# A transformer block pair on one core: later loads in the opening, and two layer-norm steps moved

## The reference, cut to what matters

```
h    = rmsnorm(x, ln_g);  proj = h @ w_in          # g_u g_v g_z | d_q d_k d_v d_z d_a d_b | c_q c_z
v    = layernorm(gelu(g_v), ln_g, ln_b)            # per position, 512 wide
s    = tril(W_s) v + b, per chunk of 128 positions and group
outa = gelu(g_u) * s * silu(g_z)
outb = rmsnorm(gated_delta_rule(q, k, v, g, beta)) * silu(d_z)          # 8 heads
m    = rmsnorm(mem, mem_norm_g);  mk, mv = m @ w_mem_kv                 # 256 memory positions
outc = softmax(c_q mk^T / sqrt(128)) mv * silu(c_z)                     # 4 heads
x    = x + [outa, outb, outc] @ w_out;  rmsnorm
```

## Time and profile before

| | us |
|---|---|
| median of 3 runs | 1923.31 (1923.17 to 1923.55) |
| the profiled execution, its own time | 1925.46 |
| its span | 1923.9 |
| PE busy | 1912.3 (99%) |
| DVE busy | 1150.7 (60%) |
| ACT busy | 816.1 (42%) |
| PE's share of the chain that ended last | 94% |
| HBM read | 193.10 MB, 105 GB/s over the span |

### The profile page before, as it was taken

One profiled execution on the slowest core, in us unless ns is written; L12 is line 12 of the kernel. 1 busy time (PEld: TensorE's weight loads), 2 busy tenths in 40 slices (PEclk: granted clock), 3 DMA queues, 4 the chain that ended last, 5 costly groups with the idle time before them and its releaser, 6 DMA issues.

```text
span 1923.9 us, 27478 instructions
## 1 busy us (share of the span) xinstructions
PE 1912.3 (99%) x9142; PEld 1590.7 (83%) x9142; DVE 1150.7 (60%) x2161; ACT 816.1 (42%) x1603; POOL 112.1 (6%) x172
## 2 busy tenths in 40 slices
PE   9999999999999999999999999999999999999999
PEld 8788888888888888888888888888888888888887
DVE  6574587788777765633655555555464646466333
ACT  5653444444444434523544343434343434344111
POOL 0100011001111010001000000000000000000100
PEclk9999999999999999999999999999999999999999
DMA  9722233223332213344332222222222222223341
GB/s 339 274 91 67 86 89 90 75 75 79 88 84 73 69 66 120 121 143 144 128 108 79 87 93 87 93 87 93 87 83 97 71 100 79 88 88 120 142 153 65
DMA packets 33737, 202.09 MB, mean 105 GB/s; under 512 B 4576, under 2 KB 4704, under 8 KB 13216
## 3 DMA queue, kind: packets, MB, share of 16 engines
q1 hardware_dynamic: 23760, 165.69, 24.2%
q0 software_dynamic: 9792, 35.76, 6.6%
q10 hardware_dynamic: 144, 0.10, 0.0%
HBM read 193.10 MB, written 8.42 MB: 105 GB/s over the span
## 4 chain that ended last, share of the span: by engine, by line
PE 94%; DVE 3%; DMA 2%; ACT 1%; issue 0%; SPq 0%; POOL 0%; DVEq 0%; ACTq 0%
PE gemm L1472 80%; PE pb L1472 12%; PE pb L1475 2%; DMA raw<-in_w 2%; DVE w_lo L823 1%; DVE act_lo L832 0%; ACT w_hi L392 0%; DVE scratch L864 0%; DVE scratch L1033 0%; DVE scratch L959 0%; DVE stat L953 0%; DVE scratch L952 0%; DVE parts L843 0%; DVE scratch L960 0%; ACT scratch L561 0%
## 5 line engine op out<-in xcount | busy, mean ns | idle before, releaser
L1472 PE MATMUL gemm<-act_hi,w_hi 128*128 128x512 f32 x2304 | 920.9, 400 | 0.2 <-DVE act_lo L832 0.2
L1472 PE MATMUL gemm<-act_lo,w_hi 128*128 128x512 f32 x2320 | 902.8, 389 | 0.2 <-DVE w_lo L823 0.2
L1472 PE MATMUL gemm<-act_hi,w_lo 128*128 128x512 f32 x2304 | 899.8, 391 | 0.0
L392 ACT ACTIVATE w_hi<-raw 128x512 fp32r<-128x512 f32 x616 | 337.0, 619 | 409.4 <-PE gemm L1472 385.9
L1472 PEld LDWEIGHTS gemm<-act_hi,w_lo 128*128 128x128 f32 x2304 | 432.4, 188 | 93.2
L1472 PEld LDWEIGHTS gemm<-act_lo,w_hi 128*128 128x128 f32 x2320 | 436.6, 188 | 83.7 <-ACT w_hi L392 0.5
L1472 PEld LDWEIGHTS gemm<-act_hi,w_hi 128*128 128x128 f32 x2304 | 433.4, 188 | 82.0 <-issue 0.8
L823 DVE TENSOR_TENSOR w_lo<-raw,w_hi 128x512 fp32r<-128x512 f32 x624 | 399.3, 695 | 142.7 <-ACT w_hi L392 135.7
L1472 PEld LDWEIGHTS pb<-scratch 128*128 128x128 f32 (+1 forms) x932 | 135.9, 190 | 31.6 <-DVE scratch L1194 5.9
L1472 PE MATMUL pb<-scratch 128*128 128x128 f32 (+4 forms) x932 | 144.9, 281 | 3.0 <-DVE scratch L838 1.8
L1342 DVE SCALAR_TENSOR_TENSOR scratch<-gemm,scratch 128x512 f32<-128x512 f32 x24 | 16.6, 691 | 150.1 <-PE gemm L1472 149.9
(11 more groups left out here) (293 smaller groups left out, 1603.2 us busy)
## 6 DMA issues: line engine op xcount, KB each, us to landing
raw<-in_w SPq DMA_DIRECT2D x154, 1024.0 KB, 4.8
scratch<-in_rows_in POOLq DMA_DIRECT2D x6, 1024.0 KB, 8.6
big<-in_xT POOLq DMA_DIRECT2D x4, 1024.0 KB, 9.4
scratch<-rows POOLq DMA_DIRECT2D x16, 256.0 KB, 6.1
scratch<-in_xT POOLq DMA_DIRECT2D x16, 256.0 KB, 3.0
x<-big POOLq DMA_DIRECT2D x16, 256.0 KB, 2.3
scratch<-x POOLq DMA_DIRECT2D x16, 256.0 KB, 4.1
outT<-scratch POOLq DMA_DIRECT2D x16, 256.0 KB, 3.7
```

Of the source, the lines that this page charges most:

```text
L392: A(w_hi[slot][:, c], raw[slot][:, c], ACT.Copy).then_inc(sem["hi"], 1)
L1472: return nc.tensor.matmul(out, a, b, start=start, stop=stop, skip_group_check=skip)
```

## The change

In POOL's opening the constants go from the end of memory block 4 (`unit` 5) to that of block 5; row copy 1 from block 4 to block 6; row copy 2 from block 5 to block 7; x's part 0 from block 6 to block 7. ACT squares row copy 1 after the conversion of unit 9 and not before that of x tiles 6 and 7; it squares copy 2 after x tiles 8 to 11, and copy 3 after the conversion of unit 10. DVE finishes the layer norm of chunks 1 and 2 after the cross-attention heads, between the steps of chunk 3.

```diff
 (POOL)
             pool.wait_ge(sem["unit"], 4)
             x_part(3)
-            pool.wait_ge(sem["unit"], 5)
+            pool.wait_ge(sem["unit"], 6)
+            pool.dma_start(cst[:, :], consts).then_inc(sem["cst_in"], 16)
+            pool.wait_ge(sem["unit"], 7)
             x_rows(1)
-            pool.dma_start(cst[:, :], consts).then_inc(sem["cst_in"], 16)
-            pool.wait_ge(sem["unit"], 6)
+            pool.wait_ge(sem["unit"], 8)
+            x_part(0)
             x_rows(2)
-            pool.wait_ge(sem["unit"], 7)
-            x_part(0)
             x_rows(3)
             x_part(1)
 (ACT)
             hi(7, 1)
             x_hi(4, 6)
             hi(U_V, 0)
-            row_squares(1)
             x_hi(6, 8)
             hi(U_V + 1, 1)
+            row_squares(1)
+            x_hi(8, 12)
             row_squares(2)
-            x_hi(8, 12)
+            hi(U_V + 2, 0)
             row_squares(3)
             act.wait_ge(sem["cst_in"], 16)
             row_scales(MT, MT + XT, XT)
-            hi(U_V + 2, 0)
             x_hi(12, KT)
 (DVE)
             v_norm(0)
             lo(U_X + 1, (U_X + 1) % 2)
             v_mean(2)
-            v_norm(1)
-            v_norm(2)
 ...
             v_poly(3)
+            v_norm(1)
             v_mean(3)
+            v_norm(2)
             v_norm(3)
```

## The result

| | before | after |
|---|---|---|
| median of 20 runs | 1923.01 us | 1926.94 us |
| lowest and highest | 1921.10, 1926.84 | 1922.38, 1928.26 |
| ratio of the times | | 1.0017 (1.0011 to 1.0023) |
| the profiled execution's span | 1923.9 | 1924.8 |

The change costs 0.17%, 3.3 us by the ratio, where 4.9 were to be won. It is outside the range and of the other sign. The two profiled executions lie 0.9 us apart; the runs further. I come to that difference with the second traces.

What follows compares the result with a forecast made beforehand. PE, busy 99% of the span, was taken to bound the kernel, so only its idle or slow time could be won. -5.24 + 1.7 - 1.4 = -4.9 us gave 1918.4 us, range 1916.4 to 1921.3.

Steps and rivals of the forecast that it cites:

- Term 1: Opening: memory block 7's wait and the slow clock behind it vanish, unit 8 starts at 53.79 not 59.03; -5.24 us.
- Term 2: Memory's scales: `negatives` issued at 73.9, not 72.50, lands later and makes PE wait; +1.7 us (0 to 3.4).
- I get 60: POOL's queue: row copy 3, waiting for ACT to square copy 1, is issued at 60.
- (b): Memory's scales: wait returns at about 3.4 us, clock may fall with it; -1.6 us, 1921.7; chance 0.13.
- (c): Copy 3 lands late; PE waits 1.7 us at x's scales, 6.1 at memory's, clock slows; +2.8, 1926.1; chance 0.06.
- Term 3: Layer norm moved off DVE before the first cross-attention head, so c_q comes sooner; -1.4 us (other end -0.7).
- (d): Opening: tile 7 stays late because something other than POOL's loads held it; -1.4 us, 1921.9; chance 0.05.
- (e): Block 7's clock drop has a cause other than the standstill; -4.9 + 1.65 us, 1920.1; chance 0.05.

Runs made afterwards that it cites:

- the second traces: One more profiled execution each of the unedited kernel before (span 1922.3 us) and the unedited changed kernel (span 1921.2 us).
- opening alone: The changed kernel with the layer-norm move undone: 1926.00 us, ratio 1.0019 to the kernel before.
- sums later: The changed kernel with ACT's wait for the small loads and its copy of the sums moved behind the conversion of unit 11: 1920.49 us, ratio 0.9990.
- ACT's old order: The changed kernel with ACT's squares at their places in the kernel before, POOL as changed: 1921.74 us, ratio 0.9998.
- sums later, ACT's old order: The changed kernel with ACT's small-load wait and sums copy behind unit 11's conversion, and ACT's squares ordered as before: 1920.52 us, ratio 0.9984.
- layer norm alone: The kernel before with only the layer-norm move: 1921.35 us, ratio 0.9996.
- the first experiments: The earlier of the follow-up kernels, timed beside the kernel before; the text doesn't list which ones.
- row copy 1 alone: The kernel before with only row copy 1 moved, from the end of memory block 4 to that of block 5: one trace, no times compared.

## Why the prediction was wrong

**Term 1, -5.24 us: the mechanism right, the size wrong.** Tile 7 landed 7.3 us after its issue in place of 11.75 (4.8 to 8.8 in all nine traces of the new opening, 9.7 to 11.7 in the four of the old one), block 7 follows block 6 without idling in every trace of the new opening, and unit 8 started at 56.0 and 54.5 in the two traces of the changed kernel. Two things were mis-sized. The base: I took the 3.42 us and the 1.65 us of slow clock of one execution for those of the median run, though its time, 1925.46, stood 2.15 us above the median, as I wrote, and put the sum on the median alike. The second trace shows 1.91 us and no slow clock. And the other end: the tiles of blocks 4 and 6, which the change doesn't touch, landed up to 2.4 us later than in the first trace, so 53.8 was reached only once. From first trace to first trace term 1 is 59.03 - 55.98 = 3.05 us, from second to second 57.18 - 54.53 = 2.65.

**Term 2, +1.7 us: the step that failed.** The place was named and so was the mechanism, but `negatives` was not issued at "73.9": it went out at 78.71, and at 76.77 in the second trace. What that number left out is the landing of row copy 2, for which the sum has no time. It lets the conversion of unit 10 (2.2 us) end at 69 behind copy 2's square (1.9 us), so it takes copy 2 to have landed by 69 - 2.2 - 1.9 = 64.9, within 10.6 us of its issue at 54.3. Copy 2 landed 13.0 us after its issue, at 70.2 (12.5 us, at 68.2, in the second trace), and it was issued later because unit 8 was late. In the traces of the new loads:

| kernel | ACT's squares | unit 8 | copy 2 issued | its square starts | last memory copy issued | `negatives` issued |
|---|---|---|---|---|---|---|
| forecast | new | 53.8 | 54.3 | | 71.8 | 73.9 |
| after, first trace | new | 55.98 | 57.16 | 70.21 | 76.61 | 78.71 |
| after, second trace | new | 54.53 | 55.74 | 68.20 | 74.66 | 76.77 |
| opening alone | new | 55.46 | 56.68 | 69.32 | 75.87 | 77.98 |
| sums later | new | 55.26 | 56.48 | 67.34 | 74.40 | 76.50 |
| ACT's old order | old | 53.75 | 54.96 | 65.73 | 72.37 | 74.48 |
| sums later, ACT's old order | old | 54.78 | 56.00 | 67.03 | 73.68 | 75.78 |

In each of them ACT stands waiting for copy 2 until it lands, and the last memory copy goes out 6.4 to 7.1 us after that square starts, in either order. "I get 60" for copy 3 was too early as well (65.19, 63.40), since copy 1's square stood behind the conversion of unit 9, whose tile landed only at 60.7. But that did not decide: in the kernel with the sums later, with the same order on ACT, copy 3 went out at 59.91, and `negatives` still at 76.50.

ACT's order has a part in it. Counted from the start of unit 8, `negatives` goes out 21.2 to 22.7 us later in the new order and 20.7 and 21.0 in the old, where I had 20.1. The times say that the old order is cheaper (0.9998 against 1.0017); why copy 2 landed sooner in it, after 9.8 to 11.0 us against 10.9 to 13.0, no run shows.

The wait was 3.0 to 3.2 us in the three traces of the new order in which the small loads are issued last and ACT waits for them, near the end of 3.4 that I had given. The forecast counts nothing for the clock behind that wait, which only (b) and (c) did; in two of the three it fell, and cost 1.7 and 3.0 us more.

**Term 3, -1.4 us: right.** Head 0 goes from 27.20 to 25.87 us in the changed kernel, and to 25.88 with the layer norm alone. The moved instructions are hidden: the gating products start at 230.38, with no idling listed before them, 118.4 us after unit 12 against 119.8 in the first trace.

**The rivals.** What happened is (b), and in the size of (c): the wait came back at the memory's scales with the slow clock. (c) had its place wrong, since x's scales never stopped PE, and its copy wrong: it was copy 2, not copy 3, that landed nearly as late as the constants had (13.0 us after its issue, against 13.9). But what followed from it, `negatives` at 78.3, is what was measured (78.71). I gave the two 0.19 together, because I weighed (b) by the middle of a landing time and took the issue time as known. (d) falls: tile 7 came sooner. (e), that the clock drop has another cause than idling, is neither shown nor needed: while PE had work, 0.50 was seen behind idling of 3.42, 3.19, 3.18 and 2.4 us, and never without; but 2.96 and 1.9 us left it at 1.00, so the length of the wait alone doesn't tell.

**The sum once more**, from first trace to first trace at unit 12: -3.05 (unit 8) + 3.5 (92.73 - 55.98 against 92.26 - 59.03) + 1.7 (clock) = +2.2; head 0 gives 1.33 back, and the spans differ by +0.9, as they do. From second to second: 108.53 - 107.94 = +0.6 at unit 12, 226.92 - 227.80 = -0.9 at the gating products, and the spans differ by -1.1. So the traces lie +0.9 and -1.1 apart where the runs lie +3.3 apart, by the ratio: most runs of the changed kernel must lose more than these traces show, as with the slow clock of the trace with the opening alone. The mean granted clock over the span, kept for each run, points the same way: it is 0.998 or 0.999 in 18 of the 20 runs of the changed kernel, the two at 1.000 are its two shortest, and in the 29 runs of the kernel before that were made beside the first experiments it is 1.000 in 23 and never 0.998. Which stretch was slow in which run was not traced.

## What to carry to other kernels

A load that is moved later takes with it every wait that stands behind it on in-order queues, so before moving one, list what shares its semaphore and what is queued behind that wait: here a copy whose result PE first reads about 150 us later (at 234.2, with the copy at 87.45) held the scales that PE was about to need, and moving two lines was worth 5.2 us. Where an engine's work is reordered to follow later loads, follow the chain load, square, slot free, next load to its end, and give every load in it a landing time, and the worst of the trace and not the middle one. And don't take the size of a stall from a single profile when that profile is dearer than the median: trace it twice.

## What the runs showed of the hardware

PE's clock adds a second cost to a wait, and not always. Waits of 2.96 and 3.19 us at the same place differ by 0.2 us, yet the first left the granted clock at 1.00 and the second was followed by 0.50 (1.2 GHz) and cost 1.7 us more; with the opening alone 3.18 us of idling were followed by 0.50 for twice as long, which cost 3.0 us; and 2.4 us with row copy 1 alone brought it too, after PE had begun again. The Trainium skill ("TensorE: Matmul & The Clock Gate", Part 1) describes the throttled clock as the state that idling brings back; every drop in these traces stands behind an idle stretch, so the trace agrees.

Loads of the same 1 MB from the same queue, with nothing changed ahead of them, landed up to 2.4 us apart between executions. Tile 6 came at 40.7 in the first trace of before, 7.2 us after its issue, and at 43.1 in that of after, 9.1 us after it. That is about as much as the later loads could win in the typical opening (2.4 to 3.4 us).
